# One recurrence of a three-layer block on Trainium2: whole transposes for the sides, values summed into u, the blocks inverted on VectorE

## The reference

```
def _rwkv_step(S, inp):
    r, w, kk, kka, kt, v = inp
    sk = einsum('bhij,bhj->bhi', S, kk)
    S = S * w[:, :, None, :] - sk[..., None] * kka[:, :, None, :] + v[..., None] * kt[:, :, None, :]
    return S, einsum('bhij,bhj->bhi', S, r)
```

## Time and profile before

| what | before |
|---|---|
| median of 3 runs | 4459.76 us (4451.9 to 4476.23) |
| the profiled execution | 4455.58 us, its span 4454.2 us |
| mean granted TensorE clock | 0.927 of full speed |
| busy over the span: PE, DVE, ACT, POOL | 89%, 34%, 23%, 28% |
| HBM read and written | 654.6 and 38.9 MB, 156 GB/s |
| instructions | 80505 |

### The profile page before, as it was taken

One profiled execution on the slowest core, in us unless ns is written; L12 is line 12 of the kernel. 1 busy time (PEld: TensorE's weight loads), 2 busy tenths in 40 slices (PEclk: granted clock), 3 DMA queues, 4 the chain that ended last, 5 costly groups with the idle time before them and its releaser, 6 DMA issues.

```text
span 4454.2 us, 80505 instructions
## 1 busy us (share of the span) xinstructions
PE 3953.2 (89%) x34715; PEld 2484.8 (56%) x34715; DVE 1495.6 (34%) x2904; ACT 1030.6 (23%) x2164; POOL 1247.1 (28%) x1239
## 2 busy tenths in 40 slices
PE   8999999998999899997999998997566676869999
PEld 7977887877887444663333333444455555433443
DVE  4333332233243220554100115024455556342223
ACT  2032111002201221551212222114333333131111
POOL 4334322423445102110011110115666567010000
PEclk9999999999999999998999999998776777889999
DMA  4254212222222212552899996226011110259999
GB/s 164 76 185 144 76 57 76 76 99 88 78 95 82 64 57 59 161 156 100 309 344 347 345 351 255 99 92 180 28 31 36 49 35 18 89 210 409 408 405 365
DMA packets 277214, 701.52 MB, mean 157 GB/s; under 512 B 27488, under 2 KB 78080, under 8 KB 276608
## 3 DMA queue, kind: packets, MB, share of 16 engines
q1 hardware_dynamic: 250608, 637.58, 38.9%
q0 software_dynamic: 26256, 58.79, 4.9%
HBM read 654.61 MB, written 38.93 MB: 156 GB/s over the span
## 4 chain that ended last, share of the span: by engine, by line
PE 30%; POOL 9%; issue 6%; DMA 5%; DVE 3%; ACT 2%; SPq 0%; POOLq 0%; DVEq 0%; ACTq 0%
PE banks L3389 9%; PE banks L2956 6%; DMA ring<-in_moe_w 4%; PE banks L3415 3%; POOL arena L1452 3%; POOL arena L1451 3%; PE banks L3399 3%; PE banks L3362 2%; PE banks L3423 1%; PE banks L3709 1%; ACT arena L1732 1%; PE banks L3498 1%; POOL ring L1430 1%; POOL ring L1428 1%; PE banks L3480 1%
## 5 line engine op out<-in xcount | busy, mean ns | idle before, releaser
L2956 PE MATMUL banks<-ring,arena 128*128 128x512 f32 x1248 | 541.8, 594 | 0.4 <-DVE arena L2440 0.4
L2997 PE MATMUL banks<-arena 128*128 128x256 f32 x2256 | 506.0, 380 | 3.2 <-DVE arena L1995 3.2
L3389 PE MATMUL banks<-ring,arena 128*64 128x512 f32 x2048 | 471.7, 600 | 13.9 <-DMA ring<-in_moe_w 8.8
L2997 PEld LDWEIGHTS banks<-arena 128*128 128x128 f32 x2256 | 435.0, 199 | 58.4 <-issue 2.7
L2956 PEld LDWEIGHTS banks<-ring,arena 128*128 128x128 f32 x1248 | 235.8, 191 | 288.8 <-issue 286.0
L2997 PE MATMUL banks<-ring,arena 128*128 128x256 f32 x1584 | 356.3, 383 | 1.6 <-DVE arena L2304 1.6
L2997 PEld LDWEIGHTS banks<-ring,arena 128*128 128x128 f32 x1584 | 314.6, 216 | 35.9 <-DVE arena L2304 2.4
L3389 PEld LDWEIGHTS banks<-ring,arena 128*64 128x64 f32 x2048 | 139.7, 137 | 327.8 <-issue 322.2
L1254 POOL TENSOR_TENSOR arena<-ring 128x1024 f32<-128x1024 f32 x47 | 117.1, 2492 | 637.2 <-PE banks L2997 621.3
L2997 PE MATMUL banks<-arena,ring 128*128 128x256 f32 x1280 | 283.0, 379 | 1.2 <-ACT arena L1584 0.7
L3415 PE MATMUL banks<-ring,arena 128*64 128x512 f32 x1024 | 259.3, 657 | 7.9 <-ACT arena L1753 6.9
(11 more groups left out here) (460 smaller groups left out, 5738.4 us busy)
## 6 DMA issues: line engine op xcount, KB each, us to landing
ring<-in_moe_w SPq DMA_DIRECT2D x768, 512.0 KB, 8.9
ring<-in_w_in SPq DMA_DIRECT2D x21, 2048.0 KB, 7.8
ring<-in_ada_w SPq DMA_DIRECT2D x12, 2048.0 KB, 8.1
ring<-in_ada_w SPq DMA_DIRECT2D x24, 1024.0 KB, 5.6
ring<-in_w_up SPq DMA_DIRECT2D x8, 2048.0 KB, 8.7
ring<-in_w_down SPq DMA_DIRECT2D x8, 2048.0 KB, 7.8
ring<-in_na_w_qkv SPq DMA_DIRECT2D x6, 2048.0 KB, 8.1
ring<-in_w_in SPq DMA_DIRECT2D x8, 1024.0 KB, 6.9
```

What stands on the lines that cost most here:

```text
L2956: ins = mm(ps[:, 0:ncol], lhs(k), rhs(k), start=(k == 0 and first), stop=(k == nk - 1))
L2997: ins = mm(ps[:, HW * j:HW * (j + 1)], lhs[:, k, j, :] if len(lhs.shape) == 4 else lhs[:, k, P * j:P * (j + 1)], rhs[:, k, :], start=(star ...
L3389: ins = mm(ps, x_chosen[:, b, k, 0:CAP_L], w[x][:, n * W:(n + 1) * W], start=(k == 0), stop=(k == KD - 1))
```

## The change

All of it is in the recurrence.

- **Sides.** `side` turns each 128x128 tile by one transpose with the full identity; the quadrant products are gone. Scaled R has a buffer for each direction, e_pos too. 
- **Values.** `solved` makes only tkT and is called `turned_keys`. `scan_u` begins with four products of the inverse with gv into the same PSUM tile, before the wait for the state, and adds the state's product to them. ScalarE copies u out, in two instructions, one for each direction's rows. tgv is gone, and there are two buffers for the inverses.
- **Row steps.** `invert_blocks` goes from GpSimd to VectorE, cut into six pieces beside steps 4 to 9 of the scan. Its scratch is a place of its own.
- **GpSimd** gets: weighing of keys, their scaling by the norms, the product of T with its decays for z = 1, the bonus values (`weigh_values`), and the last three instructions of the read-out. `factors` has other four instructions, with no scalar additions.
- **ScalarE** sums the squares: 12 instructions for the keys and 8 for the read-out, each of 64 columns with an accumulator, both at step 6.
- **Order.** One function `beside` behind the scan's part of a step. Both directions' sums and decays of m are made at steps 7 to 10 (before: one at steps 9 and 10, the other at steps 0 and 1 of the next iteration), K, R and the masked ends of m at steps 10 and 11.
- **SP.** The load of k stands ahead of w0 and w1; ln_rows has one buffer instead of two, loaded a pair at a time behind the read-out; for the last pair this load, with its wait, stands ahead of the second half of w_o. 
- In the last iteration the output products of the first half are spread over steps 5 to 10, four each (before: six each at steps 6 to 9).

```diff
+                load_pair("k", m)
                 sp.wait_ge(sem("rw_scaled"), rw_scaled(n, "B", 0))
                 load_pair("w0", m)
-                full(sp, "rw_side", n, "sum_ex", 1)
+                sp.wait_ge(sem("rw_scaled"), rw_scaled(n, "B", 1))
...
-                load_pair("k", m)
                 sp.wait_ge(sem("rw_bonus_weighed"), n + 1)
                 load_pair("rows", m)
-                sp.wait_ge(sem("rw_scaled"), rw_scaled(n, "R", 1))
                 load_pair("r", m)
+                sp.wait_ge(sem("rw_scaled"), rw_scaled(n, "T", 0))
                 load_pair("a0", m)
-                sp.wait_ge(sem("rw_scaled"), rw_scaled(n, "T", 1))
+                sp.wait_ge(sem("rw_factors"), factored(n, "scaled T1"))
                 load_pair("a1", m)
             if p >= 1:
                 sp.wait_ge(sem("rw_read_out"), p)
-                load_pair("g", n)
-                load_pair("ln", n)
+                load_pair("ln", p)
+                if n < RW_PAIRS:
+                    load_pair("g", n)
 
         def experts(l):
 
...
+        def weigh_keys(p):
+
+            loaded(pool, "k", p)
+            loaded(pool, "rows", p)
+            if p >= 1:
+                pool.wait_ge(sem("rw_blocks_turned"), p)
+            G.tensor_tensor(kk, RW_IN["k"], across(rw_rows[:, 0, :], NT), ALU.mult).then_inc(sem("rw_keys_weighed"), 1)
+
+        def scale_keys(p):
+
+            pool.wait_ge(sem("rw_key_scales"), p + 1)
+            keys = kk.rearrange("p t (h d) -> p (t h) d", d=HD)
+            G.tensor_tensor(keys, keys, rw_s[:, 0:12].unsqueeze(2).to_broadcast([P, 12, HD]), ALU.mult).then_inc(sem("rw_keys_ready"), 1)
+            pool.wait_ge(sem("rw_keys_ready"), p + 1)
+
+        def weigh_keys_by(p, z):
+
+            loaded(pool, f"a{z}", p)
+            full(pool, "rw_side", p, "sum_ex", z)
+            G.tensor_tensor(RW_IN[f"w{z}"], kk, RW_IN[f"a{z}"], ALU.mult).then_inc(sem("rw_factors"), 1)
+            pool.wait_ge(sem("rw_factors"), factored(p, f"B{z}"))
...
         def factors(p, z):
 
-            az, B, k_a = RW_IN[f"a{z}"], (RW_IN["w0"], bh[p % 2][1])[z], rw_rows[:, 1, :]
-            loaded(pool, f"a{z}", p)
-            if z == 0:
-                loaded(pool, "k", p)
-                loaded(pool, "rows", p)
-                pool.wait_ge(sem("rw_keys_ready"), p + 1)
-                full(pool, "rw_side", p, "sum_ex", 0)
-            elif p >= 2:
+            az, k_a = RW_IN[f"a{z}"], rw_rows[:, 1, :]
+            link(G.tensor_tensor(az, az, across(k_a, NT), ALU.mult))
+            link(G.tensor_tensor(az, az, across(k_a, NT), ALU.subtract))
+            link(G.tensor_tensor(az, az, RW_IN["k"], ALU.mult))
+            G.tensor_tensor(az, az, RW_IN["k"], ALU.add).then_inc(sem("rw_factors"), 1)
+            pool.wait_ge(sem("rw_factors"), factored(p, f"T{z}"))
+
+        def scale_values(p):
+
+            taken(pool, "rw_side", p, "sum", 1)
+            if p >= 2:
                 full(pool, "rw_y", p - 2, RW_STEPS - 1, 1)
-            G.tensor_tensor(B, kk, az, ALU.mult).then_inc(sem("rw_factors"), 1)
-            pool.wait_ge(sem("rw_factors"), factored(p, "B", z))
-            link(G.tensor_scalar(az, az, -1.0, None, ALU.add))
-            link(G.tensor_tensor(az, az, across(k_a, NT), ALU.mult))
-            link(G.tensor_scalar(az, az, 1.0, None, ALU.add))
-            G.tensor_tensor(az, az, RW_IN["k"], ALU.mult).then_inc(sem("rw_factors"), 1)
...
+        weigh_keys(0)
+        scale_keys(0)
+        for z in range(2):
+            weigh_keys_by(0, z)
+        for z in range(2):
+            factors(0, z)
+        for p in range(-1, RW_PAIRS):
+            n, m = p + 1, p + 2
+            if n < RW_PAIRS:
+                weigh_bonus(n)
+                scale_values(n)
+            if m < RW_PAIRS:
+                weigh_keys(m)
+                scale_keys(m)
+            if p >= 1:
+                read_out(p - 1)
+            if m < RW_PAIRS:
+                for z in range(2):
+                    weigh_keys_by(m, z)
+            if p >= 0:
+                weigh_values(p)
+            if m < RW_PAIRS:
+                for z in range(2):
+                    factors(m, z)
+        read_out(RW_PAIRS - 1)
...
 
+        def sums_of_squares(to, x, kept, n):
+
+            for i in range(n):
+                t, h = divmod(i, 2)
+                ins = A(kept[:, t, h * HD:(h + 1) * HD], x[:, t, h * HD:(h + 1) * HD], ACT.Square, accum_out=to[:, i:i + 1])
+            link(ins)
+
         def key_norms(p):
-            act.wait_ge(sem("rw_kk_squared"), p + 1)
+            act.wait_ge(sem("rw_keys_weighed"), p + 1)
+            if p >= 1:
+                act.wait_ge(sem("rw_scaled"), rw_scaled(p - 1, "T", 0))
+            sums_of_squares(rw_s[:, 0:12], kk, e_pos[0], 12)
             A(rw_s[:, 12:24], rw_s[:, 0:12], ACT.Sqrt).then_inc(sem("rw_kk_norm"), 1)
 
         def read_out_norms(p):
-            act.wait_ge(sem("rw_y_var"), p + 1)
-            A(rw_s[:, 32:40], rw_s[:, 24:32], ACT.Sqrt).then_inc(sem("rw_y_std"), 1)
+            act.wait_ge(sem("rw_y_centred"), p + 1)
+            sums_of_squares(rw_s[:, 40:48], yd[1], yd[0], 8)
+            A(rw_s[:, 32:40], rw_s[:, 40:48], ACT.Sqrt, scale=1.0 / HD, bias=c_own[:, 4:5]).then_inc(sem("rw_y_std"), 1)
...
@@ -1859,6 +1909,12 @@
 
         def scan(p, i):
 
+            ps = two_banks(full(act, "rw_u", p, i), P)
+            for z in range(2):
+                _, c = rw_chunk(i, z)
+                rows = slice(c * CH, (c + 1) * CH)
+                ins = A(u[rows], ps[rows, z], ACT.Copy)
+            free(ins, "rw_u", p, i)
             for z in range(2):
                 t, c = rw_chunk(i, z)
...
+        def invert_blocks(p, lo, hi):
+
+            if lo == 1:
+                dve.wait_ge(sem("rw_blocks_turned"), p + 1)
+            for j in range(lo, hi):
+                shape = [P, j, SUB - 1 - j]
+                rest = Y[:, 0:j, j + 1:SUB]
+                kept = arena[:, kept_at:kept_at + j * (SUB - 1 - j)].rearrange("p (c r) -> p c r", c=j)
+                link(V.tensor_tensor(kept, Y[:, j:j + 1, j + 1:SUB].to_broadcast(shape), Y[:, 0:j, j:j + 1].to_broadcast(shape), ALU.mult))
+                link(V.tensor_tensor(rest, rest, kept, ALU.subtract))
...
                 nt = LT if kind == "R" else NT
-                ps = two_banks(ps, nt * CH)
-                pe.wait_ge(sem("rw_scaled"), rw_scaled(p, kind, z))
+                if (kind, z) == ("T", 1):
+                    pe.wait_ge(sem("rw_factors"), factored(p, "scaled T1"))
+                else:
+                    pe.wait_ge(sem("rw_scaled"), rw_scaled(p, kind, z))
                 for t in range(nt):
-                    for hd, c, to, rows in quadrants:
-                        ins = mm(ps[to, c, t * CH:(t + 1) * CH], x[rows, t, to], ident[rows, rows], start=True, stop=True)
+                    ins = turn(ps[:, t * P:(t + 1) * P], x[:, t, :], ident[:, :])
...
         def scan_u(p, i):
 
+            k = i // 2
+            g, j = divmod(k, RW_TILES)
+            taken(pe, "rw_gv", p, g)
+            taken(pe, "rw_tk", p, g)
+            ps = two_banks(open_("rw_u", p, i), P)
+            for hd in range(2):
+                d = slice(hd * CH, (hd + 1) * CH)
+                for z, t, c, rows in scan_rows(i):
+                    mm(ps[rows, z, d], inverse_of(p, g)[rows, 2 * hd + j, z * CH:(z + 1) * CH], gv[rows, g, z, j, d], start=(hd == 0), stop=False)
             pe.wait_ge(sem("rw_state_ready"), state_of(p, i))
-            taken(pe, "rw_tk", p, i // (2 * RW_TILES))
-            ps = open_("rw_u", p, i)
             for z, t, c, rows in scan_rows(i):
-                ins = mm(ps[rows, 0:P], tkT[:, c, i // 2, z, :], state_at(i, z), start=True, stop=True)
+                ins = mm(ps[rows, z, :], tkT[:, c, k, z, :], state_at(i, z), start=False, stop=True)
             close(ins, "rw_u", p, i)
```

The order of the pieces on VectorE:

```diff
+        def beside(p, i):
 
             n, m = p + 1, p + 2
-            goes_on = n < RW_PAIRS
+            goes_on, follows = n < RW_PAIRS, m < RW_PAIRS
             if i == 0 and goes_on:
                 scale(n, "B", 0)
+                scale(n, "B", 1)
+            elif i == 1 and p >= 1:
+                centre(p - 1)
+            elif i == 2 and goes_on:
                 scale(n, "T", 0)
-                mask_ends(n, 0)
-            elif i == 1 and goes_on:
-                scale(n, "B", 1)
-                scale(n, "K", 1)
-                mask_ends(n, 1)
-            elif i == 2:
-                if goes_on:
-                    scale(n, "R", 1)
-                    sum_bonus(n)
-                if p >= 1:
-                    read_out(p - 1, 1)
+                mask_lead(n)
             elif i == 3 and goes_on:
                 mask_tail(n)
-            elif i == 4:
+            elif i == 4 and goes_on:
+                sum_bonus(n)
+                invert_blocks(n, 1, 7)
+            elif i == 5 and goes_on:
+                invert_blocks(n, 7, 12)
```

(60 more changed lines are left out.)

582 lines of the change are left out of this document (261 added, 321 removed).

## The result

The changed kernel takes 4475.61 us, the median of 20 runs (4467.65 to 4484.25). The kernel before, run beside it on the same chip, takes 4463.27 (20 runs, 4445.76 to 4476.23). The ratio is 1.003, with a 95% interval of 1.002 to 1.004: 0.3% slower, within the 0.5% that I called no change. The profiled execution is 4469.69 us against 4455.58 before. The medians further down are of all executions, the ratios leave out the few far slower ones (10020.66 us in e3, 6839.07 in e10, 16735.53 once beside e1 to e4).

What follows compares the result with a forecast made beforehand. No engine is full: each pair is a ring of waits, 90.3 us. Back half 52.6 plus front half 32 make 84.6, seven times -40; with ends -7.5, -47 in all, giving a median of 4413 us, range 4370 to 4482.

Steps and rivals of the forecast that it cites:

- Front half after, 32 us: From the end of the VectorE transposes to step 4's state product: 32 us instead of 43.4, range 29 to 37.
- Back half after, 52.6: From step 4 to the end of the next transposes: VectorE's queue 42.3, wait for u 3.3, port waits 7.
- Turned sides, 0: TensorE's sides: 44 whole turns for 352 matmuls a pair at about equal time, 0 gained, bounds -2 to +3.
- Values in u, 0: Values computed inside u, ScalarE copying u out: the longer step chain hides under VectorE's queue, so it costs nothing.
- Row steps, 21.9 us on VectorE: Inversion's 30 row steps, 60 instructions a pair: 21.9 us on VectorE against 39.5 on GpSimd.
- Ends: Outside the steady pairs: -7.5 us up to pair 0's transposes (0 to -15), 0 for the last pair.
- Rival 2: The ring stays as long, through a lower TensorE clock or slower pieces: no change, 4455 us, chance 0.2.
- The ScalarE piece: Squares, two roots and table load on ScalarE at step 6: 6.8 us, delaying u by 3.3 at step 7.
- Its third element: No change also follows if the front half takes 35 us and the step 6 squares cost their whole 6.8.
- Rival 1: GpSimd instructions block VectorE's row steps throughout: +5 us a pair, 4490 us; chance 0.15 together with rival 4.
- Rival 4: Early decays go unused, front half keeps 43 us, period 95.6; chance 0.15 together with rival 1.
- rival 3: Rows run in GpSimd's pauses, ScalarE's squares are covered, stalls fall: 77 to 80 us a pair, 4372 us, chance 0.11.

Runs made afterwards that it cites:

- e3: Changed kernel with the read-out's eight squares and root moved from step 6 to step 5 on ScalarE; 4452.00 us, ratio 0.9974 to the kernel before.
- e10: Changed kernel with the 48 products of the off blocks issued twice in step 2; 4500.23 us, ratio 1.0085 to the kernel before.
- e1: Changed kernel with GpSimd's factor and read-out operations cut to one of 16 columns each; 4435.08 us, ratio 0.9939 to the kernel before.
- e4: Changed kernel with the row steps on GpSimd again, behind its scaling of the values; 4560.17 us, ratio 1.0217 to the kernel before.
- e13: Changed kernel with TensorE's values of the third group and ScalarE's copy of them moved from step 0 to step 3; 4486.59 us, ratio 1.006.
- e7: Changed kernel with the sides turned by four 64x64 products a tile again; 4477.22 us, ratio 1.0031 to the kernel before.
- e8: Kernel before with only the sides turned by whole 128x128 transposes; 4450.64 us, ratio 0.9978 to the kernel before.
- e14: Changed kernel with the solved values u copied out by VectorE again instead of ScalarE; 4501.20 us, ratio 1.0088 to the kernel before.
- e15: Changed kernel with the row steps on GpSimd again and the weighing of the next keys ahead of them; 4448.62 us, ratio 0.9967.
- e5: Changed kernel with the third group's mask ahead of the other VectorE work of step 8; 4489.30 us, ratio 1.0059 to the kernel before.

## Why the prediction was wrong

I forecast 4413 us and gave "faster" 0.62; the kernel stayed within 0.5%, on the slow side, inside the range of 4370 to 4482. By its own steps:

*Front half after, 32 us: this step failed.* It came to 38.8, and 6.8 of the 7.8 us between the forecast period and the measured one are here. The sum followed VectorE's queue. In the pair at 3529 us its first member held (state of step 0 done at 11.8 us against 11.7), then step 1 ended at 20.6 (17.2), step 2 at 27.4 (22.8), and the stretch from there to step 4 took 13.8 us where I had put 9.2. TensorE's own pieces in steps 0 and 1 (values of the third group 1.97, sides and join) were not in the sum. Neither were its low clock in this half (0.59 in this pair) and, in steps 2 and 3, 6.1 us of stalls in which it waits for instructions (4.2 a pair on average), of which the earlier trace rows had shown one of 1.29. The kernel before had them too, so they should have been taken over into the sum. e10 and e13 show TensorE on the path there. How the 6.8 us divide among these pieces no run shows. e1 shows that the factors at the port, for which I had widened the range to 37, are worth 1 us.

*Back half after, 52.6: near.* Measured 53.7 on average. In the pair at 3570 us, where it is 56.6, the excess of five row steps in step 8 is 5.5 us (7 forecast), and the wait behind the squares 4.8 (3.3), which cancel. VectorE idled another 3.5 us that the sum did not have: 2.2 for state products behind other copies, 1.3 for the rb products. Its own work with the gaps in it, some 43 us, was near the 42.3.

*Turned sides, 0:* right, -0.6 a pair (e7, e8). *Values in u, 0:* not tried as a whole. Of its two halves e14 tests one, the engine of the copy, and VectorE would cost 4.7 a pair more. *Row steps, 21.9 us on VectorE:* right. They are 25.1 us busy a pair, averaged over six pairs, of which 5.3 are excess of instructions beside GpSimd's; 19.8 and the 2.4 between them make 22.2. The error was to take for granted that 39.5 - 21.9 is a gain. On GpSimd the rows ran beside VectorE's other work and through its waits. On VectorE every wait (for the port, behind the squares) is added to a full queue: 53.7 against 45.1 (e15).

*Ends.* First pair: the stretch from the first decay sum to the last transpose became 2.9 us shorter, not 7.5. Last pair: -2.0 behind the last memset against 0; TensorE waited 2.9 us for the output weights where I had 6.

*Rivals.* Rival 2 gave the result, but by neither of its ways. The clock over a pair went from 0.74 to 0.73 (from 0.68 to 0.62 in the front half, from 0.79 to 0.82 in the back half), and the form of the turns is not the cause (e7, e8). The ScalarE piece cost 4.8 of its 6.8. Its third element, a front half of 35 or more, is what happened. Rival 1 named a real mechanism that stayed small in the steady pair and shows in full in e5. Rival 4's longer front half did not occur.

*Small slips in the prediction.* By its own terms rival 1 gives 4493 us against the median (4455.6 + 33.5 + 4.2), not 4490, and rival 3 gives 4375, not 4372. GpSimd runs 21 instructions a pair in the changed kernel, not 20. None of this changes the forecast.

## What to carry over

When an engine is relieved, sum the new ring over every engine, the one that only takes part included: here TensorE had 26 us of work and 15 of waits in a half that I had written as VectorE's. Take over every stall that the old timeline shows, also one put down to issue alone. Before a block of small instructions goes onto an engine that also makes a copy on the path, look at what stands in front of that copy. Moving eight squares by one step was worth more (2.9 us a pair) than several of the parts of the change. And price the first round of a pipeline apart, as an order that gains 1 us in each later pair cost 18 in the first.

## What the hardware showed that I had not expected

VectorE and GpSimd, both with two SBUF operands, take turns instruction by instruction: a 30-column row step of 0.2 us lasts 1.85 beside 768-column multiplies of 1.80 (e5). TensorE runs out of instructions in long runs of 32-column products: it stands still for up to 5.7 us, and each of 192 stalls of over 0.9 us ends 1.2 to 1.7 us behind the end of a 16384-byte packet of the instruction queue, with or without other DMAs under way. Doubling 48 such products raised the stalls from 24.4 to 40.2 us over the seven pairs (e10), and with quarter turns in place of whole ones, more instructions for the same result, they are 32.4 (e7). And a granted clock has to be averaged before it is compared: the back halves of the changed kernel alone lie between 0.76 and 0.92.
